# The boundary between two sub-layers: output tail by column halves, squares and gating by halves, another order of rounding

## The reference

```python
def ffn_sublayer(x, shift, scale, gate, g_pre, g_post, w_in, w_out):
    h = modulate(rmsnorm(x, g_pre), shift, scale)
    a, b = jnp.split(h @ w_in, 2, axis=-1)
    h = (jax.nn.silu(a) * b) @ w_out
    return x + FFN_RES * gate * rmsnorm(h, g_post)
```

## Time and profile before

| | |
|---|---|
| median of 3 runs | 3286.37 us (3283.35 to 3288.7) |
| profiled execution | 3282.8 us |
| its span | 3280.9 us |
| TensorE busy | 3083.7 us, 94% of the span |
| VectorE busy | 2155.5 us, 66% |
| ScalarE busy | 1139.0 us, 35% |
| GpSimd busy | 575.8 us, 18% |
| mean granted clock | 0.971 |

### The profile page before, as it was taken

One profiled execution on the slowest core, in us unless ns is written; L12 is line 12 of the kernel. 1 busy time (PEld: TensorE's weight loads), 2 busy tenths in 40 slices (PEclk: granted clock), 3 DMA queues, 4 the chain that ended last, 5 costly groups with the idle time before them and its releaser, 6 DMA issues. The chain is left out here.

```text
span 3280.9 us, 48857 instructions
## 1 busy us (share of the span) xinstructions
PE 3083.7 (94%) x19610; PEld 2836.7 (86%) x19610; DVE 2155.5 (66%) x2879; ACT 1139.0 (35%) x1941; POOL 575.8 (18%) x578
## 2 busy tenths in 40 slices
PE   6999879999999999999999997679999999979999
PEld 5999758999899998998999997468998999868998
DVE  4777486777776657776876535647777877585444
ACT  3222454223422424223322433234224222454222
POOL 1112101112111111112111102642112112201001
PEclk8999999999999999999999998679999999999999
DMA  7666414666565446665665443024664766313443
GB/s 267 199 206 185 146 43 134 198 217 190 184 196 173 115 123 192 193 211 168 206 205 149 128 127 98 15 68 156 216 201 148 225 203 204 112 43 95 126 127 97
DMA packets 565510, 515.80 MB, mean 157 GB/s; under 512 B 42965, under 2 KB 499238, under 8 KB 563494
## 3 DMA queue, kind: packets, MB, share of 16 engines
q1 hardware_dynamic: 565286, 512.68, 51.0%
HBM read 509.37 MB, written 3.24 MB: 156 GB/s over the span
## 5 line engine op out<-in xcount | busy, mean ns | idle before, releaser
L1342 PE MATMUL bank<-h_hi,w_hi 128*128 128x384 f32 x3328 | 1116.8, 336 | 3.8 <-DVE tmp L1801 3.8
L1344 PE MATMUL bank<-h_hi,w_lo 128*128 128x384 f32 x3328 | 1114.8, 335 | 0.0
L1343 PE MATMUL bank<-h_lo,w_hi 128*128 128x384 f32 x3328 | 1114.2, 335 | 0.0
L1757 DVE TENSOR_TENSOR w_lo<-raw,w_hi 128x1024 fp32r<-128x1024 f32 x648 | 804.1, 1267 | 411.8 <-ACT w_hi L1603 406.9
L1603 ACT ACTIVATE w_hi<-raw 128x1024 fp32r<-128x1024 f32 x648 | 679.1, 1059 | 1015.7 <-PE bank L1375 483.8
L1779 DVE SCALAR_TENSOR_TENSOR fold<-ada_raw,cond,fold 128x1024 f32<-128x1024 f32 x462 | 638.5, 1438 | 0.0
L1342 PEld LDWEIGHTS bank<-h_hi,w_hi 128*128 128x128 f32 x3328 | 625.6, 188 | 12.9 <-DVE tmp L1801 6.0
L1343 PEld LDWEIGHTS bank<-h_lo,w_hi 128*128 128x128 f32 x3328 | 625.5, 188 | 5.8
L1344 PEld LDWEIGHTS bank<-h_hi,w_lo 128*128 128x128 f32 x3328 | 625.3, 188 | 0.0
L2069 POOL TENSOR_TENSOR h_lo<-tmp,h_hi 128x384 fp32r<-128x384 f32 x176 | 284.9, 1619 | 1786.5 <-DVE h_hi L1805 1786.5
L1371 PE MATMUL bank<-w_hi,h_hi 128*128 128x512 f32 x1056 | 334.4, 398 | 0.0
(11 more groups left out here) (200 smaller groups left out, 2512.0 us busy)
## 6 DMA issues: line engine op xcount, KB each, us to landing
raw<-w_ffn_in SPq DMA_DIRECT2D x352, 512.0 KB, 5.0
ada_raw<-w_ada SPq DMA_DIRECT2D x272, 512.0 KB, 4.2
raw<-w_ffn_out SPq DMA_DIRECT2D x176, 512.0 KB, 4.8
raw<-w_hgrn_in SPq DMA_DIRECT2D x40, 512.0 KB, 4.7
g_rows<-g_dram SPq DMA_DIRECT2D x12, 1024.0 KB, 6.8
raw<-w_attn_qkv SPq DMA_DIRECT2D x24, 512.0 KB, 5.3
raw<-w_conv_in SPq DMA_DIRECT2D x24, 512.0 KB, 4.9
ada_first<-w_ada SPq DMA_DIRECT2D x16, 512.0 KB, 10.6
```

Source lines behind the costliest of these rows:

```text
L1342: mm(out, wh, h_hi[:, k, :], start=(k == 0), stop=False)
L1343: mm(out, wh, h_lo[:, k, :], start=False, stop=False)
L1344: last = mm(out, wl, h_hi[:, k, :], start=False, stop=(k == DC - 1))
L1757: V.tensor_tensor(w_lo[:, b % RING, :], raw[:, b % RAW, :], w_hi[:, b % RING, :].bitcast(F32), ALU.subtract).then_inc(w_lo_made, 1)
```

## The change

In the tail, TensorE finishes a tile by column halves: all four chunks of half 0, then all four of half 1 (`out_half` in place of `out_tile`; the other output blocks take their products in this order too, three in a row into one bank). The signal `acc_done` is given per half. ScalarE squares each half as it comes, VectorE gates each half after its square. The transposes of tile 0 stand behind the first chunk of half 0 of the last tile. ScalarE modulates half 0 of tile 1 before it squares y of the last tile. VectorE rounds half 0 of tile 1 before y's last variance, and half 1 of tile 1 only between `hi_last(e, 0)` and `hi_last(e, 1)`. GpSimd starts on the low parts when the last tile is normalised instead of when tile 1 is rounded. The unread products move to bank 7 and change in number: 8 to 10 or 16 to 18 before the transposes of the last tile, 4 to 1 after them, and the fold's rows are turned after these products.

```diff
--- before.py
+++ after.py
@@ -1234,6 +1234,10 @@
     def columns(n):
         return slice(n * D // 2, (n + 1) * D // 2)
 
+    def acc_number(s, t, n):
+
+        return (2 * NT - 1) * s + 2 * t + n + 1
+
 
     @blk.sync
     def _(sp):
@@ -1365,16 +1369,12 @@
                               start=False, stop=(k == DC - 1))
                 last.then_inc(block_done, 1)
 
-        def out_tile(b, t, hi, lo, opens, closes):
-
-            for n in range(2):
-                mm(psum[2 * t + n][:, :], hi[:, tokens(t)], w_hi[:, b % RING, columns(n)], start=opens, stop=False)
-            for n in range(2):
-                mm(psum[2 * t + n][:, :], hi[:, tokens(t)], w_lo[:, b % RING, columns(n)], start=False, stop=False)
-            for n in range(2):
-                last = mm(psum[2 * t + n][:, :], lo[:, tokens(t)], w_hi[:, b % RING, columns(n)], start=False,
-                          stop=closes)
-            return last
+        def out_half(b, t, n, hi, lo, opens, closes):
+
+            out = psum[2 * t + n][:, :]
+            mm(out, hi[:, tokens(t)], w_hi[:, b % RING, columns(n)], start=opens, stop=False)
+            mm(out, hi[:, tokens(t)], w_lo[:, b % RING, columns(n)], start=False, stop=False)
+            return mm(out, lo[:, tokens(t)], w_hi[:, b % RING, columns(n)], start=False, stop=closes)
 
         def moving_out(s, c):
 
@@ -1395,7 +1395,8 @@
             out_ready(s, c)
             hi, lo = moving_out(s, c)
             for t in range(NT):
-                last = out_tile(b, t, hi, lo, c == 0, False)
+                for n in range(2):
+                    last = out_half(b, t, n, hi, lo, c == 0, False)
                 if t == 1 and between is not None:
                     between()
             last.then_inc(block_done, 1)
@@ -1412,24 +1413,25 @@
         def unread_products(n):
 
             for _ in range(n):
-                mm(psum[6][:, 0:P], ident, ones[:, :], start=True, stop=True)
+                mm(psum[7][:, 0:P], ident, ones[:, :], start=True, stop=True)
 
         def out_tail(s, chunks, b):
 
             e = s + 1
             for t in range(NT):
-                for n, c in enumerate(chunks):
-                    if t == 0:
-                        pe.wait_ge(w_lo_made, b + n + 1)
-                        out_ready(s, c)
-                    hi, lo = moving_out(s, c)
-                    last = out_tile(b + n, t, hi, lo, False, n == TAIL - 1)
-                    if t == NT - 1:
-                        last.then_inc(block_done, 1)
-                        if n == 0 and e < N_SUB:
+                for n in range(2):
+                    for i, c in enumerate(chunks):
+                        if t == 0 and n == 0:
+                            pe.wait_ge(w_lo_made, b + i + 1)
+                            out_ready(s, c)
+                        hi, lo = moving_out(s, c)
+                        last = out_half(b + i, t, n, hi, lo, False, i == TAIL - 1)
+                        if t == NT - 1 and n == 1:
+                            last.then_inc(block_done, 1)
+                        if t == NT - 1 and n == 0 and i == 0 and e < N_SUB:
                             turn_normed(e, 0)
-                if t < NT - 1:
-                    last.then_inc(acc_done, 1)
+                    if t < NT - 1 or n == 0:
+                        last.then_inc(acc_done, 1)
             if e < N_SUB:
                 turn_normed(e, 1)
                 if late_fold(s) is not None:
@@ -1437,16 +1439,16 @@
                     pe.wait_ge(a_read, FC * ffn_number(e))
                     pe.wait_ge(b_read, FC * ffn_number(e))
                     fold_up(late_fold(s), 6)
+                    unread_products(10)
                     ada_turn(late_fold(s), 7)
-                    unread_products(8)
                 else:
                     if sub_kind[s] == "ffn":
-                        pe.wait_ge(a_read, FC * (ffn_number(s) + 1))
-                    unread_products(16)
+                        pe.wait_ge(b_read, FC * (ffn_number(s) + 1))
+                    unread_products(18)
                 turn_normed(e, 2)
-                unread_products(4)
                 if late_fold(s) is not None:
                     pe.wait_ge(mods_made, late_fold(s) + 1)
+                unread_products(1)
 
         def ada_half(half, bank, slab):
 
@@ -1649,20 +1651,17 @@
             for c in range(DC - TAIL):
                 split(b0 + n_in + c + 6)
 
-        def out_squares(e, t):
+        def out_squares(e, t, n):
 
             s = e - 1
-            if t < NT - 1:
-                act.wait_ge(acc_done, (NT - 1) * s + t + 1)
+            if t < NT - 1 or n == 0:
+                act.wait_ge(acc_done, acc_number(s, t, n))
             else:
                 act.wait_ge(block_done, first_block[e])
-            for n in range(2):
-                if n == 1:
-                    act.wait_ge(og_made, 2 * (NT * s + t) + 1)
-                number = square_number(e, t, n, False)
-                act.wait_ge(squares_made, number - 2)
-                A(junk[number % 3], psum[2 * t + n][:, :], ACT.Square, scale=1.0 / 32,
-                  accum_out=o_ss[:, 2 * t + n:2 * t + n + 1]).then_inc(squares_made, 1)
+            number = square_number(e, t, n, False)
+            act.wait_ge(squares_made, number - 2)
+            A(junk[number % 3], psum[2 * t + n][:, :], ACT.Square, scale=1.0 / 32,
+              accum_out=o_ss[:, 2 * t + n:2 * t + n + 1]).then_inc(squares_made, 1)
 
         def y_squares(e, t):
 
@@ -1689,23 +1688,28 @@
             last.then_inc(hf_high if half else hf_low, 1)
 
         def boundary(e):
-            if e > 0:
-                out_squares(e, 0)
-                y_squares_after(e, 0)
-                out_squares(e, 1)
-                if e < N_SUB:
-                    modulate(e, 0, 0)
-                y_squares_after(e, 1)
-                out_squares(e, 2)
-                if e < N_SUB:
-                    modulate(e, 0, 1)
-                    if late_fold(e - 1) is not None:
-                        ada_copy(2 * late_fold(e - 1), 6)
-                    y_squares_after(e, 2)
-                    modulate(e, 1, 0)
-                    modulate(e, 1, 1)
-                    modulate(e, 2, 1)
-                    modulate(e, 2, 0)
+            if e == N_SUB:
+                for t in range(NT):
+                    out_squares(e, t, 0)
+                    out_squares(e, t, 1)
+            elif e > 0:
+                out_squares(e, 0, 0)
+                out_squares(e, 0, 1)
+                y_squares(e, 0)
+                out_squares(e, 1, 0)
+                out_squares(e, 1, 1)
+                modulate(e, 0, 0)
+                y_squares(e, 1)
+                out_squares(e, 2, 0)
+                modulate(e, 0, 1)
+                out_squares(e, 2, 1)
+                modulate(e, 1, 0)
+                y_squares(e, 2)
+                if late_fold(e - 1) is not None:
+                    ada_copy(2 * late_fold(e - 1), 6)
+                modulate(e, 1, 1)
+                modulate(e, 2, 1)
+                modulate(e, 2, 0)
             else:
                 for t in range(NT):
                     y_squares(e, t)
@@ -1721,10 +1725,6 @@
             if e < N_SUB:
                 for b in range(2, 6):
                     split(first_block[e] + b)
-
-        def y_squares_after(e, t):
-            if e < N_SUB:
-                y_squares(e, t)
 
         def turn_copy(n, dst, src):
             act.wait_ge(turn_done, n + 1)
@@ -1838,19 +1838,13 @@
             V.tensor_scalar(var[:, t:t + 1], ss[:, 2 * t:2 * t + 1], EPS, ss[:, 2 * t + 1:2 * t + 2], ALU.add,
                             ALU.add).then_inc(made, 1)
 
-        def gated(e, t, halves):
+        def gated(e, t, n):
 
             s = e - 1
-            if t < NT - 1:
-                dve.wait_ge(acc_done, (NT - 1) * s + t + 1)
-            else:
-                dve.wait_ge(block_done, first_block[e])
             dve.wait_ge(g_landed, 16 * e)
-            for n in halves:
-                if n == 0:
-                    dve.wait_ge(squares_made, square_number(e, t, 0, False) + 1)
-                V.tensor_tensor(og[:, t % 2, columns(n)], psum[2 * t + n][:, :], g_rows[:, group_of(t), columns(n)],
-                                ALU.mult).then_inc(og_made, 1)
+            dve.wait_ge(squares_made, square_number(e, t, n, False) + 1)
+            V.tensor_tensor(og[:, t % 2, columns(n)], psum[2 * t + n][:, :], g_rows[:, group_of(t), columns(n)],
+                            ALU.mult).then_inc(og_made, 1)
 
         def out_variance(e, t):
 
@@ -1925,36 +1919,39 @@
                 lo_last(e, 1)
                 lo_last(e, 0)
             elif e < N_SUB:
-                gated(e, 0, (1, 0))
+                gated(e, 0, 0)
                 out_variance(e, 0)
+                gated(e, 0, 1)
                 residual(e, 0)
+                gated(e, 1, 0)
                 y_variance(e, 0)
                 normed(e, 0)
```

(17 more changed lines are left out.)

## The result

The changed kernel takes 3269.19 us (median of 5, 3267.81 to 3271.1) against 3286.37 us (3283.35 to 3289.21) before: a ratio of 0.9949, 95% interval 0.9938 to 0.996. The forecast was 3270 us. Run again on another occasion it took 3267.95 us against 3284.46, ratio 0.995 (0.9936 to 0.9963). One execution of a kernel further down, `tile0_by_chunks`, took 7807.82 us where its others took 3256.55 to 3258.86; it is left out of that ratio.

A forecast was written before the change was run, and what follows sets the result against it. TensorE, busy 94% of the span, bounds the kernel, idling at 11 boundaries and the end. Four mixer boundaries (6.7 us), seven FFN ones (9.2) and the end (0.37) give 16.3 us: 3270 us, range 3264 to 3275, with rivals to 3279.

The forecast's parts named there:

- Part 1: At each boundary, squaring the last tile by halves lets its variance follow sooner: 1.27 us saved.
- Part 2: At each boundary, `hi_last` no longer stands behind the rounding of tile 1: 1.13 us saved (0.8 to 1.3).
- Parts 3 and 4: Added waits: 0.57 us before tile 0's transposes at each boundary, 0.36 us for the fourth chunk at 8 FFN tails.
- Part 5: Before the low products, VectorE and GpSimd share ports: TensorE waits 0 to 0.5 us, taken as 0.15.
- the first count: Low parts at a boundary, three kinds of work one after another: 6.3 us after GpSimd's start; TensorE arrives at 6.57.
- The second count: Low parts at a boundary, by bare lengths with the port held strictly: 6.96 us after GpSimd's start, a 0.5 us wait.
- Part 6: Unread products before the last tile's transposes, late fold and product order cost nothing; 18 unread products are covered by 0.4 us.
- Part 4: At 8 FFN tails, tile 0 wants the fourth chunk after 9 products instead of 18: 0.36 us wait each.
- A: All 3744 output products pay for the same bank in a row; at 10 ns each, 3307 us; chance 0.05.
- B: At 8 FFN tails VectorE gets in before GpSimd's subtraction, costing 0.9 us more each: 3277 us; chance 0.08.
- C: Behind boundaries, loads keep their own pace; four mixers and some FFN starts keep half: 3278 us; chance 0.10.
- D: At boundaries `hi_last` finds another wait or the CAST delays it; 12.4 us go: 3282.4 us, no change; chance 0.10.

The follow-up runs named there:

- tile0_by_chunks: `variance_first` with tile 0 of the tail worked off chunk by chunk again, both halves: 3258.19 us, ratio 0.9914; run again 3257.71 us, 0.9916.
- variance_first: The changed kernel with `y_variance(e, 0)` ahead of `gated(e, 1, 0)` on VectorE: 3260.09 us, ratio 0.9924 to the kernel before.
- blocks_alternate: The changed kernel with output blocks outside the tail alternating between a tile's two banks again: 3269.35 us, ratio 0.9951 to the kernel before.
- halves_alone: The changed kernel with the old order behind the last tile's squares (modulation and rounding of tile 1, GpSimd's start): 3284.78 us, ratio 0.9998.
- lows_late: The changed kernel with GpSimd's old wait, starting the low parts only when tile 1 is rounded: 3286.96 us, ratio 1.0003 to the kernel before.

## Why the prediction was right, step by step

| step | predicted | measured |
|---|---|---|
| last product to the last tile's transposes, saved | 1.27 us | 1.27 (6.76 to 5.49) |
| `hi_last` behind them, saved | 1.13 us | 1.08 (1.78 to 0.70) |
| transposes of tile 0 wait | 0.57 us | 0.67 to 0.76 by `variance_first`, 1.02 at boundary 2 |
| FFN tail waits for its fourth chunk | 0.36 us | 0.46 by `tile0_by_chunks` |
| low parts wait | 0.15 us (0 to 0.5) | none |
| a boundary behind an FFN | 1.32 us | 1.13 (no fold) to 1.18; 1.18 to 1.23 by the second profiles |
| a boundary behind a mixer | 1.68 us | 1.63 to 1.68, but 1.29 at boundary 2 |
| the end of the kernel | 0.37 us | 0.24 to 0.27 |
| whole | 16.3 us | 17.2 and 16.5 (medians) |

The order of events was right at every step, and the part that the sum had largest came as forecast. *Part 1*: the variance starts 0.92 us behind the last product, where 0.9 to 1.0 was named. *Part 2*: 0.05 us short of the estimate for four transposes. *Parts 3 and 4*: both waits came where they were expected and both were taken too small, by 0.16 and 0.10 us. What was missing is for the most part the restart: the products behind a wait come 0.07 to 0.08 us late each time, beside the gap itself (0.63 and 0.37 us from start to start, less a product's pitch). That the first wait is the same everywhere was wrong for boundary 2. *Part 5*: the low parts cause no wait. VectorE is through with its two subtractions at 2992.93, 6.34 us behind GpSimd's start, as the first count had it (6.3). TensorE comes to them at 2993.31, 5.66 us behind its first product; the sum took 5.54, though its own rows have 5.66 as well (2998.71 to 3004.37). So up to 0.38 us are to spare. The second count, one operation after another at bare lengths, gave 6.96 us and a wait of 0.5: it is too long by 0.6. The rule in the Trainium skill ("SBUF — State Buffer", "Who interferes with whom"), that whoever issues first holds the shared pair of ports for the whole instruction while the other blocks, was put beside that count. On the hold itself the trace agrees: a CAST that comes second takes 1.23 or 1.24 us, one that comes first 0.42. *Part 6* cost nothing: 18 unread products end before the transposes, and TensorE still stands idle for 0.43 us.

In the first pair of profiles the 7 boundaries behind an FFN give 8.2 us, the 4 behind a mixer 6.3 and the end 0.2: 14.7 us, and 15.0 in the second pair, of 16.5 to 17.2 measured in the medians. The forecast of 16.3 was too high in the steps by 1.3 to 1.6 us, and that it came so near to the medians is in part luck. Where the remaining 1.5 to 2.5 us come from is open; the two pairs of profiles give 11.7 and, with the second ones, 16.3 us between the spans (3281.6 and 3265.3), so single executions can't tell.

One bound of the prediction doesn't follow from its terms: parts 2 and 5, off by what it names at 11 places, reach from 3265 to 3277 us when both go the same way, not from 3264 to 3275. Part 4 comes to 0.34 us by its own working, not 0.36. Neither changes the reading.

The rivals: A is refuted by `blocks_alternate`. B did not come: GpSimd's subtraction takes 1.02 us at the tails. C, that the gain is given back behind the boundary, is seen at one place, the second attention, and nowhere in the FFNs by more than their spread. That loads are the reason, as C had it, is not shown; what goes with it there is the granted clock. D did not come, but `halves_alone` shows that it is what would have happened had the order not been changed with the halves.

One assumption behind the sum fell, and the total didn't show it, since both parts were changed together. It added parts 1 and 2 as if each could be had by itself. Alone they give 0 and 1.6 us. The gap on ScalarE that takes up the modulation of tile 1 is made by the halves; the prediction said that the modulation was moved and never asked whether there was room for it.

Two small moves on top give a kernel that beats both: `y_variance(e, 0)` ahead of the gating of tile 1, and tile 0 by chunks, 3257.7 us, 0.9916 (0.9903 to 0.993) of the kernel before.

## What to carry to other kernels

When a path crosses engines that work in program order, list for each engine what stands in front of the instruction that the path needs; here a gating of 0.6 us in front of a variance of 0.2 cost 8 us over 11 boundaries, and swapping two lines brought it back. Finishing a result by halves shortens the path behind it, but it also asks for the last input sooner: look up when that input is ready before choosing the order. Parts of one change may be worth nothing apart, so test them together and apart before one is dropped.

## What the hardware showed that I had not expected

A wait cost TensorE more than the idle time that is recorded in front of it: 0.73 us against 0.47 at the transposes (`variance_first`), 0.46 against 0.20 at the FFN tails (`tile0_by_chunks`).

A later start of GpSimd moved its end by more than the shift. In `lows_late` it started 2.1 us later, and its four subtractions took 5.92 us instead of 5.19, as they then ran beside both of VectorE's, so it ended 2.8 us later. The kernel lost 18 to 19 us by that one wait at 11 boundaries.

In the second attention, twelve profiles of these kernels fall into two kinds, 153.9 to 155.0 us at a granted clock of 0.96 and 155.4 to 156.1 at 0.93 or 0.95. A gain of 1.6 us at the boundary behind it doesn't show in the distance between boundaries when the kind changes too.
